# Forty products of a three-layer kernel in halves of 128 columns, and an earlier wait for the bias masks

## The reference, cut to what matters

```python
def first_block(x, ...):                      # two layers
    for layer in range(2):
        u = rms_norm(h, g_mix[layer])
        h = h + (mla_stick_breaking_mixer if layer == 0 else chunk_band_mixer)(u, ...)
        u = rms_norm(h, g_ffn[layer])
        h = h + (silu(u @ w_gate) * (u @ w_up)) @ w_down       # D_FF = 2816
    return rms_norm(h, g_final)

# chunk_band_mixer: 16 heads of 64; chunks of 64 tokens
    bias = rel_bias[:, clip(rel, -256, 256) + 256]
    scores = q @ k.T * 64 ** -0.5 + bias       # later chunks are masked
    o = softmax(scores) @ v;  return o @ w_out

def second_block(x, ...):                     # 16 meta tokens ahead: 272 rows
    proj = rms_norm(stream) @ w_in             # conv, q, k, v, index q and k, gates
    stream += (g_a * conv_branch + g_b * top_k_attention) @ w_merge_out
    stream += (silu(a) * b) @ ffn_down         # after a 3-wide convolution of h @ ffn_up
    return rms_norm(stream)[16:]
```

## Time and profile before

| what | us |
|---|---|
| three runs | 1073.36, 1072.09, 1073.35 |
| median | 1073.35 |
| the profiled execution | 1074.75 |
| its span, first to last instruction | 1073.0 |
| PE busy | 1056.7 (98%), 8777 matmuls |
| DVE, ACT, POOL busy | 754.6, 576.0, 207.5 |

### The profile page before, as it was taken

One profiled execution on the slowest core, in us unless ns is written; L12 is line 12 of the kernel. 1 busy time (PEld: TensorE's weight loads), 2 busy tenths in 40 slices (PEclk: granted clock), 3 DMA queues, 4 the chain that ended last, 5 costly groups with the idle time before them and its releaser, 6 DMA issues.

```text
span 1073.0 us, 22189 instructions
## 1 busy us (share of the span) xinstructions
PE 1056.7 (98%) x8777; PEld 1024.1 (95%) x8777; DVE 754.6 (70%) x1238; ACT 576.0 (54%) x853; POOL 207.5 (19%) x189
## 2 busy tenths in 40 slices
PE   9999999999999999999999999999999999999997
PEld 8998899999999889999999999999899999999997
DVE  6778665555757776655655589987988668887652
ACT  5668554444545555644455454446668355565532
POOL 0432030000210000300000287885450000000000
PEclk9999999999999999999999999999999999999999
DMA  9735356656675443566545745553335535654451
GB/s 278 218 111 173 104 188 190 191 169 213 222 239 176 139 157 96 184 194 195 176 159 197 234 121 172 153 184 118 115 123 166 185 123 190 196 187 149 163 173 40
DMA packets 187940, 181.31 MB, mean 169 GB/s; under 512 B 17951, under 2 KB 186284, under 8 KB 187867
## 3 DMA queue, kind: packets, MB, share of 16 engines
q1 hardware_dynamic: 187179, 177.94, 52.4%
q0 software_dynamic: 544, 2.10, 0.7%
q10 hardware_dynamic: 144, 0.26, 0.1%
HBM read 179.24 MB, written 1.05 MB: 168 GB/s over the span
## 4 chain that ended last, share of the span: by engine, by line
PE 88%; DVE 6%; ACT 4%; issue 2%; POOL 1%; DVEq 0%; ACTq 0%
PE ps L575 27%; PE ps L576 27%; PE ps L580 27%; DVE w_lo L397 2%; ACT w_hi L381 1%; DVE ps L2716 1%; PE ps L1882 1%; PE ps L2056 1%; PE ps L2249 1%; PE ps L2065 1%; POOL w_lo L409 1%; PE ps L1851 0%; PE ps L1803 0%; PE ps L1875 0%; PE ps L1863 0%
## 5 line engine op out<-in xcount | busy, mean ns | idle before, releaser
L397 DVE TENSOR_TENSOR w_lo<-raw,w_hi 128x2048 fp32r<-128x2048 f32 (+3 forms) x157 | 333.3, 2137 | 138.9 <-ACT w_hi L381 138.7
L381 ACT ACTIVATE w_hi<-raw 128x2048 fp32r<-128x2048 f32 (+3 forms) x182 | 316.5, 1754 | 32.1 <-PE ps L580 22.1
L575 PE MATMUL ps<-u_hi,w_hi 128*128 128x256 f32 x944 | 264.8, 281 | 0.4 <-DVE w_lo L2437 0.4
L576 PE MATMUL ps<-u_lo,w_hi 128*128 128x256 f32 x944 | 261.4, 277 | 0.0
L580 PE MATMUL ps<-u_hi,w_lo 128*128 128x256 f32 x940 | 260.3, 277 | 0.0
L575 PE MATMUL ps<-m_hi,w_hi 128*128 128x258 f32 (+2 forms) x792 | 227.2, 287 | 1.2 <-POOL w_lo L409 0.5
L576 PE MATMUL ps<-m_lo,w_hi 128*128 128x258 f32 (+2 forms) x792 | 223.7, 282 | 0.0
L580 PE MATMUL ps<-m_hi,w_lo 128*128 128x258 f32 (+2 forms) x792 | 223.7, 282 | 0.0
L575 PEld LDWEIGHTS ps<-u_hi,w_hi 128*128 128x128 f32 x944 | 177.7, 188 | 3.0 <-issue 1.9
L576 PEld LDWEIGHTS ps<-u_lo,w_hi 128*128 128x128 f32 x944 | 177.3, 188 | 0.2
L580 PEld LDWEIGHTS ps<-u_hi,w_lo 128*128 128x128 f32 x940 | 176.6, 188 | 0.0
(11 more groups left out here) (368 smaller groups left out, 1617.8 us busy)
## 6 DMA issues: line engine op xcount, KB each, us to landing
raw<-in_w_in SPq DMA_DIRECT2D x24, 1024.0 KB, 5.4
raw<-in_w_gate SPq DMA_DIRECT2D x22, 1024.0 KB, 5.3
raw<-in_w_up SPq DMA_DIRECT2D x22, 1024.0 KB, 5.4
raw<-in_ffn_up SPq DMA_DIRECT2D x22, 1024.0 KB, 5.1
raw<-in_w_down SPq DMA_DIRECT2D x16, 768.0 KB, 4.7
raw<-in_od_w_qkv SPq DMA_DIRECT2D x12, 1024.0 KB, 5.2
raw<-in_w_down SPq DMA_DIRECT2D x16, 640.0 KB, 4.9
raw<-in_ev_w_in SPq DMA_DIRECT2D x7, 1024.0 KB, 10.5
```

Source lines behind the costliest of these rows:

```text
L381: nc.scalar.activation(w_hi[t % RING][:, 0:n], raw[t % RAW][:, 0:n], ACT.Copy).then_inc(hi_done, 1)
L397: nc.vector.tensor_tensor(w_lo[t % RING][:, 0:n], raw[t % RAW][:, 0:n], w_hi[t % RING][:, 0:n].bitcast(F32), ALU.subtract).then_inc(lo_don ...
L575: nc.tensor.matmul(out_ap, a_h, b_h, start=start and n == 0, stop=False)
L576: nc.tensor.matmul(out_ap, a_h, b_l, start=False, stop=False)
```

## The change

`product` gets `halved` true at more places: one slice of the first tile in the first units of stages and behind attention steps, in the middle of tiles, so that further matmuls are added to the same PSUM tile behind it; in the down stages it is the last slice of the first tile in each unit with k % 4 < 2. Per execution that makes 1 in the first unit, 2 in units 1 and 2, 4 in `out0`, 1 in `ffn0`, 8 in `down0`, 1 in `qkv`, 4 in `out1`, 1 in `ffn1`, 8 in `down1`, 2 in the mixing stage's index queries (`qi`) and 8 in `down2`: 40. And GpSimd's bias masks wait for five finished `w_lo` of `down0` in place of `xl_done`.

```diff
--- before.py
+++ after.py
@@ -625,7 +625,7 @@
                 for t in range(2):
                     cols = slice(t * P, (t + 1) * P)
                     mm = product(outs[t], [(hi[:, kt, cols], lo[:, kt, cols], xh(kt), xl(kt))],
-                                 kt == 0, kt == KT - 1)
+                                 kt == 0, kt == KT - 1, n == T1 and (t, kt) == (0, 5))
         mm.then_inc(unit_done, 1)
 
     def down_unit(name, ph, i, k):
@@ -636,7 +636,8 @@
             nc.tensor.wait_ge(sem("ffn_lo"), 2 + FFN[name] + (k0 + nk + 1) // 2)
         for t in range(2):
             mm = feature_tile(ps[:, 2 * p + t, 0:T1], s, nk, UC, t * P, lambda kt: a_hi[:, kt, :],
-                              lambda kt: a_lo[:, kt, :], x0=k0, start=k % 4 == 0, stop=k % 4 == 3)
+                              lambda kt: a_lo[:, kt, :], x0=k0, start=k % 4 == 0, stop=k % 4 == 3,
+                              halved=t == 0 and k % 4 < 2)
             if ph is ph_down2 and k == ph.units - 1 and t == 0:
                 mm.then_inc(sem("down_half"), 1)
         mm.then_inc(unit_done, 1)
@@ -1257,7 +1258,7 @@
                           ap=[[1, P], [513, t.shape[1]], [1, 2 * P]])
             nc.gpsimd.dma_start(t, rel).then_inc(sem("bias_landed"), 16)
         pool.wait_ge(sem("bias_landed"), 32)
-        pool.wait_ge(sem("xl_done"), split_at["mix1"] + 2)
+        pool.wait_ge(lo_done, ph_down0.u0 + 5)
         for n, t in enumerate(biases):
             own = t[:, :, 0:P]
             nc.gpsimd.tensor_tensor(own, own, c("chunk_mask")[:, ::-1].unsqueeze(1).to_broadcast([P, t.shape[1], P]), ALU.add)\
@@ -1939,7 +1940,8 @@
             pe.wait_ge(sem("xl_done"), split_at["mix0"] + kt + 1)
             for t in range(2):
                 cols = slice(t * P, (t + 1) * P)
-                mm = product(fm_bank(0, t), [(hi[:, kt, cols], lo[:, kt, cols], uh(kt), ul(kt))], kt == 0, kt == KT - 1)
+                mm = product(fm_bank(0, t), [(hi[:, kt, cols], lo[:, kt, cols], uh(kt), ul(kt))], kt == 0, kt == KT - 1,
+                             (t, kt) == (0, 6))
         mm.then_inc(unit_done, 1)
 
         def block_unit(k, x, tokens):
@@ -1953,7 +1955,7 @@
                         terms = (u_hi[:, kt, cols], u_lo[:, kt, cols], hi[:, kt, :], lo[:, kt, :])
                     else:
                         terms = (hi[:, kt, cols], lo[:, kt, cols], uh(kt), ul(kt))
-                    mm = product(fm_bank(k, t), [terms], kt == 0, kt == KT - 1)
+                    mm = product(fm_bank(k, t), [terms], kt == 0, kt == KT - 1, k < 3 and (t, kt) == (0, 5))
             mm.then_inc(unit_done, 1)
 
         for k in range(1, 9):
@@ -2000,18 +2002,18 @@
                         mm = product(ps[:, FM_BANKS[12][b], :],
                                      [(lat_hi[:, 3 + kt, rows], lat_lo[:, 3 + kt, rows], hi[:, kt, :], lo[:, kt, :])], kt == 0, kt == 1)
             mm.then_inc(unit_done, 1)
-        def out0_group(k, kt, t):
+        def out0_group(k, kt, t, halved=False):
             s = (ph_out0.u0 + k) % RING
             hi, lo = pw(w_hi[s], KT, UC), pw(w_lo[s], KT, UC)
             cols = slice(t * P, (t + 1) * P)
             return product(fm_bank(13 + k, t), [(hi[:, kt, cols], lo[:, kt, cols], o_hi[:, kt, :], o_lo[:, lo_tile(kt), :])],
-                           kt == OUT0_ORDER[0], kt == OUT0_ORDER[-1])
+                           kt == OUT0_ORDER[0], kt == OUT0_ORDER[-1], halved)
 
         def out0_part(k, j, t, x=None):
             if x is not None:
                 fm_steps(x)
             pe.wait_ge(sem("xl_done"), split_at["o0"] + j + 1)
-            return out0_group(k, OUT0_ORDER[j], t)
+            return out0_group(k, OUT0_ORDER[j], t, (k, j, t) in ((0, 3, 0), (2, 3, 0), (0, 7, 0)))
 
         for k in range(2):
             fm_begin(13 + k)
@@ -2042,7 +2044,7 @@
         fm_begin(16)
         for t in range(2):
             for kt in OUT0_ORDER:
-                mm = out0_group(3, kt, t)
+                mm = out0_group(3, kt, t, t == 0 and kt == OUT0_ORDER[5])
         mm.then_inc(unit_done, 1)
         ffn_pe(ph_ffn0, T1, "ffn0")
         down_pe("ffn0", ph_down0)
@@ -2109,7 +2111,7 @@
                             terms = (hi[:, kt, cols], lo[:, kt, cols], uh(kt), ul(kt))
                         else:
                             terms = (u_hi[:, kt, cols], u_lo[:, kt, cols], hi[:, kt, :], lo[:, kt, :])
-                        mm = product(out[:, t, :], [terms], kt == 0, kt == KT - 1)
+                        mm = product(out[:, t, :], [terms], kt == 0, kt == KT - 1, k == 1 and (t, kt) == (0, 5))
             mm.then_inc(unit_done, 1)
             if k == 0:
                 late_sums("mix1")
@@ -2120,12 +2122,12 @@
                     mm = nc.tensor.transpose(ps[:, 7, b * P:(b + 1) * P], rstd[:, b * P:(b + 1) * P], ident)
                 mm.then_inc(sem("tok_turned"), 1)
 
-        def out1_group(k, kt, t):
+        def out1_group(k, kt, t, halved=False):
             s = (ph_out1.u0 + k) % RING
             hi, lo = pw(w_hi[s], KT, UC), pw(w_lo[s], KT, UC)
             cols = slice(t * P, (t + 1) * P)
             return product(out1_bank(k, t), [(hi[:, kt, cols], lo[:, kt, cols], o3_hi[:, kt, :], o3_lo[:, kt, :])],
-                           kt == 0, kt == KT - 1)
+                           kt == 0, kt == KT - 1, halved)
 
         pairs_read_after = [ph_qkv.used_after[n] for n in range(3)]
         for k in range(3):
@@ -2144,7 +2146,7 @@
                 for kt in range(KT - 2):
                     ck_steps(ck_start(12 + k) + t * (KT - 2) + kt)
                     pe.wait_ge(sem("xl_done"), split_at["o1"] + kt + 1)
-                    out1_group(k, kt, t)
+                    out1_group(k, kt, t, (t, kt) == (0, 4))
         for kt in (KT - 2, KT - 1):
             pe.wait_ge(sem("xl_done"), split_at["o1"] + kt + 1)
             for k in range(3):
@@ -2158,7 +2160,7 @@
         pe.wait_ge(sem("ck_ptc"), C_H)
         for t in range(2):
             for kt in range(KT):
-                mm = out1_group(3, kt, t)
+                mm = out1_group(3, kt, t, (t, kt) == (0, 5))
         mm.then_inc(unit_done, 1)
         ffn_pe(ph_ffn1, T1, "ffn1")
         down_pe("ffn1", ph_down1)
@@ -2289,7 +2291,8 @@
             def by_features(T, t, kt):
                 cols, at = MIX_COLS.get(kind, C2), slice(t * P, (t + 1) * P)
                 return product(mix_bank(T, cols.stop - cols.start),
-                               [(hi[:, kt, at], lo[:, kt, at], m_hi[:, kt, cols], m_lo[:, kt, cols])], kt == 0, kt == KT - 1)
+                               [(hi[:, kt, at], lo[:, kt, at], m_hi[:, kt, cols], m_lo[:, kt, cols])], kt == 0, kt == KT - 1,
+                               kind == "qi" and (t, kt) == (0, 4))
 
             def by_tokens(out_ap, kt, tokens, cols):
                 return product(out_ap, [(m_hi[:, kt, tokens], m_lo[:, kt, tokens], hi[:, kt, cols], lo[:, kt, cols])],
```

## The result

The changed kernel takes 1076.26 us in the median of 8 runs (1075.43 to 1076.66), the kernel before 1073.05 beside it (8 runs, 1071.94 to 1074.55). The ratio is **1.0031**, with an interval of 1.0021 to 1.0040: slower by 0.3% (3.21 us by the medians), and above the forecast range. The profiled execution of after took 1076.64 us around a span of 1074.8.

What follows compares the result with a forecast made beforehand. TensorE's instruction starts, at two paces, bound the kernel. Halves +4.94, mask step -2.46 and slow stretches ended -2.39 make +0.09 us; with 1.40 less from the profiled 1074.75 to the median, 1073.4 us, range 1072.0 to 1074.6.

Steps and rivals of the forecast that it cites:

- so 1.40 less: Last step of the sum: the median run lies 1.40 us below the profiled execution's 1074.75 us.
- the mask step: GpSimd's bias masks in down0 start 3.3 us earlier; the stall at 275.70 goes and fast follows: -2.46 us.
- 40 more halved products: Count per execution, eight in each of three down stages and 16 elsewhere; 38 were charged at 0.13 us, +4.94.
- The price: On TensorE, each halved product costs 0.13 us for its second weight load, between 0.113 and 0.14.
- rival 5: On TensorE, the second weight load hides entirely, saving 38 x 0.13: 1068.4 us; chance 0.04.
- Fast follows: Behind a halved product TensorE steps at the fast pace, 113.3 ns, not the slow 117.8.
- rival 1: Halves toggle TensorE's pace, so those met in fast leave slow: 1074.7, or 1078.6 us in the FFN stages; chance 0.10.
- rival 2: Halves don't set TensorE's pace at all; price and mask step stay: +2.5, 1075.8 us; chance 0.08.
- The gain of the halves met in slow: First units, output stages and last down stage: each saves 4.43 ns per product until the next interruption, -2.39 us together.
- One ahead of a stall is free: Two halves right before stalls another engine ends, as at 402.93, cost nothing, or 0.13 us each without that cover.
- Rival 3: In down0, a bias landing over 0.8 us later keeps the w_lo stall and slow: +1.2, 1074.6 us; chance 0.10.
- Rival 4: Fast is handed on through attention steps, up to -1.8: 1071.6 us, or 1071.0 with cheaper halves; chance 0.17.

Runs made afterwards that it cites:

- e1: The kernel before, run again without any edit: 1073.21 us, ratio 1.0001 to the kernel before beside it.
- e8: The kernel before, profiled a third time without any edit: 1072.09 us in one run.
- e4: The changed kernel without the ten halved products in later turns of the two FFN loops, so with 40: 1074.39 us, ratio 1.0012 to the kernel before.
- e7: The kernel before with a halved product in both tiles of all 16 down units of down1, 32 in all: 1077.33 us in one run.
- e3: The kernel before with all 50 new halved products of the change but the old wait of the masks: 1076.14 us, ratio 1.0023.
- e12: The kernel before with its existing halved product in unit 3 left whole, in the FFN stages of layers 1 and 2: 1084.73 us in one run.
- e5: The kernel before with the new mask wait and two halved products, in out0's first unit and out1's last: 1070.90 us, ratio 0.9987.
- e2: The kernel before with only the wait of the bias masks changed, no new halved product: 1072.12 us, ratio 0.9987.
- e11: The kernel before with only ten new halved products, in the first unit of every later turn of two FFN loops: 1074.36 us in one run.
- e6: The kernel before with halved products among products of 258 columns, six in ffn2 and one in wo: 1073.24 us in one run.

## Why the prediction was wrong

Two steps failed. The one is the last of the sum, **"so 1.40 less"**. It took the distance of 1.40 us between the profiled execution and the median for something that any kernel has. It wasn't: that execution had drawn slow in `down0` (62.09 for 60.67) and in `down2` (71.63 for 70.34). Of the times of the kernel before in three groups of runs, 69 in all, the highest is 1074.67, so the profiled one, 1074.75, lay above them all. The sum credited the change with ending just these slow stretches, 1.64 in `down0` and 0.24 + 0.38 + 0.38 in `down2`, and then went down by the 1.40 as well, though a median run has less of them: the fast draws of e1 and e8 took 1071.82 and 1072.09, the medians of before in the three groups 1072.88 to 1073.01, so about 1 us of slow stretches is left in them where the profiled one had 2.7. (No profile shows a median run; this is an estimate from those times.) So much of the gain stood in the forecast twice. For 40 halved products and the mask step it had 0.09 us more than the profiled execution; e4 is 1.38 above the median of before beside it. Against its own base, 1074.75 + 0.09 = 1074.84 us was the forecast for 40 halved products, and e4, which has 40, measured 1074.39.

The other is **the count: "40 more halved products"**. There are 50. The branch under `ready` was read as that of a stage's first unit, and it is that of each turn's. Ten times 0.13 us were missing, 1.36 by the stages of after and e4, 1.87 by their medians. From the forecast's own 1073.44, e4 with its 40 products is 0.95 away, inside the range, and after is 1.87 beyond e4; so by this split the count weighs more, though 0.51 of the 1.87 is not accounted for by the ten products. Putting either right would have left the result inside: without the 1.40, the range moves up to 1072.2 to 1077.1; with ten more products at 0.13, to 1072.1 to 1077.0.

The other steps, one by one:

- *The price, 0.13 us, bounds 0.113 to 0.14.* Right: 0.124 over 32 and 0.127 over eight. The second down stage should be about 1.0 us longer, and is 1.02 longer. That it is the second weight load which costs, and not the second matmul as such, no run separates. The estimate from the Trainium skill ("TensorE: Matmul & The Clock Gate", Back-to-back issue gap) was 3 to 53 ns for the extra matmul; the runs with more halves speak against that, with 124 and 127 ns, as the trace of before did, and rival 5 falls with it.
- *Fast follows.* Right for all but one place: the groups of the down stages in after and e7 are at 276 and 277, and rival 1, the toggle, falls. The exception is the one halved product in which the activations are the stationary operand and the weights the moving one, in unit 2 of the first stage. It is met in slow and leaves slow: 16 steps from 26.92 to 28.81 us in after, 118 ns each, and the same in e3 and e4. The forecast had 0.08 us from it.

```profile
26.58 0.33 PE L570 MATMUL ps<-w_hi,u_lo 128*128 128x128 f32 x2
26.92 0.28 PE L576 MATMUL ps<-w_lo,u_hi 128*128 128x256 f32 x1
...
28.81 0.28 PE L580 MATMUL ps<-w_hi,u_lo 128*128 128x256 f32 x1
```

- *Halves set the pace.* Right but for that place, and e12 is the test: rival 2 falls. What in a halved product does it, the second load or the 128 columns, was not tried.
- *The gain of the halves met in slow.* In `out0`, whose gain reaches into `ffn0`, it came at least as counted: the two take 155.81 us in e4 for 156.05, 0.24 less, where five halves at 0.13 less 0.60 make +0.05. In `out1` it didn't: `out1` and `ffn1` take 150.12 in e4, 0.17 to 0.25 more than in before and e1, where four paid halves less 0.45 make +0.07. The halved product at 425.13 turned the pace, but the `w_lo` of `ffn1`'s unit 1 took the gain (see e5). In `down2` the forecast's 1.00 was there only against a slow draw: 71.43 us in after, for 71.63 and for 70.34. Groups from 419.8 and from 425.9 us in after:

```profile
L576 PE MATMUL ps<-o_lo,w_hi 128*128 128x256 f32 x16 | 4.5, 281 | 0.0
...
L576 PE MATMUL ps<-o_lo,w_hi 128*128 128x256 f32 x9 | 2.5, 276 | 0.0
```

- *One ahead of a stall is free.* Right. In after the stall of the earlier trace rows still ends where VectorE ends it, and is shorter by what the halved product takes:

```profile
402.91 0.33 PE L570 MATMUL ps<-o_hi,w_lo 128*128 128x128 f32 x2
403.86 0.39 PE L575 MATMUL ps<-o_hi,w_hi 128*128 128x256 f32 x1 [0.61 <-DVE o_lo L2636]
```

- *The mask step.* Its mechanism was right, and in e2, without the halves, so are its times: the masks start at 267.65. In after they are 1.8 us later than forecast. They start at 269.62, not 267.8: the second bias DMA is issued 1.2 us later (257.82 for 256.63), since TensorE reaches the stage later (253.94 for 252.69, of which 0.55 is a later first unit in this execution and the rest halves), and the masks start 11.8 us behind that issue, not 11.1. The row that the prediction calls "all in SBUF" reads only SBUF but writes to `ps`, so it was no row of `u_lo`'s kind; that `u_lo` waits for the mask and the eviction doesn't is shown by after's own rows above (3.33 us, 0.76). Rival 3, the `w_lo` that is met again, didn't come, and in e2, with no halves ahead, the stall is gone as well.
- *Rival 4, fast handed on through attention steps.* Not seen: `qkv` took 85.14 us for 85.15, and the first stage of layer 1 none less either (85.14 for 84.87).

Still open is what draws the pace behind a stall or an attention step; the stall's own rows in before and in e1 are the same to 10 ns.

## What to carry to other kernels

When the profiled execution isn't a typical one, find out by which stages it differs, from a second profile of the same program, before a gain in one of them is counted; a distance to the median is not an offset. Count what an edit adds by running through the loops that reach the edited line, turn by turn, and not by the name of the branch. And an edit that resets a state is worth its price only where the bad state is nearly certain and long; here the stages show that for one of the 50 new places, in `out0`, besides those that the kernel had. A gain ahead of a wait counts only up to that wait: in `out1` the reset worked and the next `w_lo` took what it gave.

## What the runs showed of the hardware

- TensorE has two paces for the same 128x256 fp32 products, 113.3 and 117.8 ns a step, in the same span with a granted clock of 0.998 to 0.999 in every run; which one follows an interruption can change from one execution to the next. The 33 runs of the kernel before beside e1 are 3 us apart (1071.66 to 1074.67). Beside after its 8 runs are 2.6 apart and those of after 1.2, which fits fewer long stretches left to chance but isn't shown to come from that.
- An interruption isn't always a draw. Behind L508 near 145 us the pace is slow in before, after, e1, e2, e7 and e12 alike, though it was fast ahead of it. Behind a halved product of 256 columns it was fast wherever a stretch of at least 12 steps follows, but for the one with the activations as the stationary operand, at 26.58 us in after, which left slow there and in e3 and e4.
- Products of 258 columns have paces of their own. A unit of 48 of them in `ffn2` takes 5.71 us in e8 and 5.76 in e11 and e12, where nothing in that stage was changed; the stage is 125.86 or 126.83 us. A halved product doesn't bring it under 125.86 (e6, where the stage was in the shorter of the two); none was met in the longer.
